# Bias table and first compress weights in 512 KB pieces, each behind a unit of the first sublayer

## The reference

```
for i in range(DEPTH):
    y = swiglu(rms_norm(h, g[0]), ffn_w_gate[i, 0], ffn_w_up[i, 0], ffn_w_down[i, 0])
    h = h + 0.5 * rms_norm(y, g[1])
    u = rms_norm(h, g[2])
    y = nsa_mixer(u, ..., rel_bias) if i % 2 == 0 else fox_mixer(u, ...)
    h = h + rms_norm(y, g[3])
    ... # second feed-forward sublayer, with g[4] and g[5]
```

## Time and profile before

| what | before |
|---|---|
| median of 3 runs | 1053.37 us (1052.19 to 1053.69) |
| the profiled execution | 1051.25 us |
| its span, first to last instruction | 1049.4 us |
| PE busy, share of the span | 98% |
| mean granted TensorE clock | 0.996 |
| HBM traffic over the span | 177 GB/s |

### The profile page before, as it was taken

One profiled execution on the slowest core, in us unless ns is written; L12 is line 12 of the kernel. 1 busy time (PEld: TensorE's weight loads), 2 busy tenths in 40 slices (PEclk: granted clock), 3 DMA queues, 4 the chain that ended last, 5 costly groups with the idle time before them and its releaser, 6 DMA issues.

```text
span 1049.4 us, 14401 instructions
## 1 busy us (share of the span) xinstructions
PE 1024.0 (98%) x5995; PEld 880.1 (84%) x5995; DVE 646.2 (62%) x777; ACT 517.7 (49%) x709; POOL 115.6 (11%) x219
## 2 busy tenths in 40 slices
PE   6989999999999999999999999999999999999997
PEld 6878888898866898888889888888988789888886
DVE  4646556656697665556575656556667775556554
ACT  4534444644465554444454444445554655444442
POOL 0100000222153200000020000001133420000000
PEclk9999999999999999999999999999999999999999
DMA  8694565568402365566556655655655145566552
GB/s 256 223 366 161 179 194 200 167 213 262 141 2 71 125 206 182 182 199 199 181 182 201 193 178 190 200 191 171 201 173 189 46 133 184 184 197 199 179 185 79
DMA packets 137830, 187.98 MB, mean 179 GB/s; under 512 B 7249, under 2 KB 120230, under 8 KB 137766
## 3 DMA queue, kind: packets, MB, share of 16 engines
q1 hardware_dynamic: 133702, 172.83, 50.9%
q0 software_dynamic: 3920, 14.18, 4.1%
q10 hardware_dynamic: 144, 0.07, 0.0%
HBM read 184.42 MB, written 1.07 MB: 177 GB/s over the span
## 4 chain that ended last, share of the span: by engine, by line
PE 88%; DVE 4%; DMA 2%; POOL 2%; ACT 2%; issue 2%; DVEq 0%; POOLq 0%; SPq 0%; ACTq 0%
PE ps L1117 85%; DMA raw<-in_ffn_w_gate 2%; PE ps L1456 1%; ACT work L527 1%; DVE normed L781 1%; POOL ms L402 1%; DVE wlo L746 1%; POOL rstd L404 1%; DVE res L770 1%; PE ps L1286 1%; DVE probT_buf L899 1%; POOL ms_half L398 0%; DVE normed L762 0%; DVE normed L877 0%; DVE wlo L738 0%
## 5 line engine op out<-in xcount | busy, mean ns | idle before, releaser
L738 DVE TENSOR_TENSOR wlo<-raw,whi 128x2048 fp32r<-128x2048 f32 x151 | 346.9, 2298 | 149.6 <-ACT whi L503 149.5
L1117 PE MATMUL ps<-xhl,whi 128*128 128x512 f32 (+1 forms) x1600 | 388.3, 385 | 3.4 <-DVE wlo L738 3.4
L1117 PEld LDWEIGHTS ps<-xhl,whi 128*128 128x128 f32 x1600 | 283.5, 189 | 54.7 <-issue 5.5
L503 ACT ACTIVATE whi<-raw 128x2048 fp32r<-128x2048 f32 x151 | 288.1, 1908 | 29.3 <-DMA raw<-in_ffn_w_gate 12.0
L1117 PEld LDWEIGHTS ps<-xhl,wlo 128*128 128x128 f32 x1600 | 216.5, 191 | 16.2 <-DVE wlo L746 1.7
L1117 PE MATMUL ps<-xhl,wlo 128*128 128x256 f32 (+1 forms) x1600 | 221.8, 282 | 0.9 <-DVE wlo L746 0.9
L1117 PE MATMUL ps<-whi,xhl 128*128 128x256 f32 (+1 forms) x640 | 136.1, 320 | 2.9 <-DVE xhl L789 2.9
L1117 PE MATMUL ps<-whi,hhi 128*128 128x512 f32 x320 | 124.9, 390 | 0.0
L1117 PE MATMUL ps<-wlo,hhi 128*128 128x512 f32 x320 | 124.9, 390 | 0.0
L1117 PE MATMUL ps<-whi,hlo 128*128 128x512 f32 x320 | 124.5, 389 | 0.0
L1117 PEld LDWEIGHTS ps<-whi,xhl 128*128 128x128 f32 x640 | 103.8, 193 | 12.3 <-DVE wlo L746 3.1
(11 more groups left out here) (169 smaller groups left out, 777.2 us busy)
## 6 DMA issues: line engine op xcount, KB each, us to landing
raw<-in_ffn_w_down SPq DMA_DIRECT2D x44, 1024.0 KB, 4.9
raw<-in_ffn_w_gate SPq DMA_DIRECT2D x41, 1024.0 KB, 5.3
raw<-in_ffn_w_up SPq DMA_DIRECT2D x41, 1024.0 KB, 5.4
raw<-in_fox_w_in SPq DMA_DIRECT2D x10, 1024.0 KB, 5.3
raw<-in_nsa_w_in SPq DMA_DIRECT2D x8, 1024.0 KB, 5.4
big<-in_nsa_cmp_w POOLq DMA_DIRECT2D x2, 2048.0 KB, 16.3
raw<-in_nsa_w_out SPq DMA_DIRECT2D x4, 1024.0 KB, 5.4
raw<-in_fox_w_out SPq DMA_DIRECT2D x4, 1024.0 KB, 4.7
```

The source lines that it names most:

```text
L503: nc.scalar.activation(whi[:, u % RING, :], raw_of(u), ACT.Copy).then_inc(w_hi, 1)
L738: nc.vector.tensor_tensor(wlo[:, u % RING, :], raw_of(u), whi[:, u % RING, :].bitcast(F32), ALU.subtract).then_inc(w_lo, 1)
L1117: return nc.tensor.matmul(out_, l, r, start=start, stop=stop)
```

## The change

POOL issues the two gain loads first, as soon as the scratch tensor has landed. The bias table is loaded in four pieces of four heads each (512 KB), piece b behind a wait for unit_done = 9, 11, 13, 15, and `w1` in four pieces of four row groups each (512 KB), behind unit_done = 17, 19, 21, 23. The two waits of the consumers count all four pieces.

```
             pool.wait_ge(vec_out, 16)
-            pool.dma_start(bias[:, :, :], bass.AP(scratch.tensor, 0, [[1, P], [SCORES, H], [1, S]])).then_inc(bias_in, 16)
             load_gain(0, 1)
             load_gain(1, 0)
-            pool.dma_start(w1, cmp_w1[0, 0].rearrange("(k p) n -> p k n", p=P)).then_inc(w1_in[0], 16)
+            for b in range(4):
+                pool.wait_ge(unit_done, 9 + 2 * b)
+                pool.dma_start(bias[:, 4 * b:4 * b + 4, :],
+                               bass.AP(scratch.tensor, 4 * b * SCORES, [[1, P], [SCORES, 4], [1, S]])).then_inc(bias_in, 16)
+            for b in range(4):
+                pool.wait_ge(unit_done, 17 + 2 * b)
+                pool.dma_start(w1[:, 4 * b:4 * b + 4, :],
+                               cmp_w1[0, 0][512 * b:512 * b + 512, :].rearrange("(k p) n -> p k n", p=P)).then_inc(w1_in[0], 16)
             between_sublayers(0)
...
                     def compressed_logits(r):
                         dve.wait_ge(sc_mm, r + 1)
-                        dve.wait_ge(bias_in, 16)
+                        dve.wait_ge(bias_in, 64)
...
             def compress_hidden(kv):
                 pe.wait_ge(flat_ready, kv + 1)
-                pe.wait_ge(w1_in[kv], 16)
+                pe.wait_ge(w1_in[kv], 16 if kv else 64)
```

## The result

The changed kernel takes 1046.09 us in the median of 6 runs (1046.0 to 1046.93), the kernel before 1052.95 in 6 runs (1050.06 to 1053.69); the ratio is 0.9941, 95% interval 0.9929 to 0.9952 (a ratio is formed over all the runs, so it is not the quotient of the two medians). The profiled execution went from 1051.25 to 1046.00 us, its span from 1049.4 to 1044.2.

What follows compares the result with a forecast made beforehand. PE sets the pace, busy in 98% of the span, but stalls for one late weight load. Idle time and slow clock, read together as 5.15 us, come off 1053.37, additions cost 0: 1048.2 us, range 1045.6 to 1050.8.

Steps and rivals of the forecast that it cites:

- The stall and its cause: First sublayer, before unit 10: POOL's 5 MB starve the ring, its load takes 15.56 us and PE idles 3.78 us.
- The yardstick of 11.8 us: Ring load of unit 10: harmless to PE if landed within 11.8 us of issue; a normal landing takes 5.3.
- The sum: Whole kernel: removing the stall saves 5.15 us, from 1051.25 to 1046.1 profiled and from 1053.37 to 1048.2 in the median.
- the clock, 1.51: First unit after the hole: PE at a mean granted clock of 0.84 takes 1.51 us more than the next unit.
- the lower bound of the range: Median: if its 2.12 us above the profiled execution were more of this stall, 7.3 us is gained, 1046.1.
- The gains on top of unit 8: Gain loads issued first, while unit 8's ring load is in flight: it lands at 8.1 us, inside 11.8, cost 0.
- The pieces beside the ring: Ring loads of units 12 to 26 issued with a piece: landing at 6.7 us, at worst 9.5, cost 0.
- The slower rival: Ring loads beside the eight pieces land after 11.8 us; at 13.0 the kernel takes 1057.8 us; chance 0.03.
- POOL's wait before the norm factors: POOL between sublayers: eighth piece issued about 146, norm factors wanted about 193, cover 47 us, cost 0.
- The price of small transfers: Eight pieces on POOL's queue: 25.6 us against 13.6 for two whole loads by the skill's estimate, where nobody waits, cost 0.

Runs made afterwards that it cites:

- e4: Kernel before with only w1, whole, moved behind unit_done 17; whole bias and gains at once as before; 1046.38 us, ratio 0.9946.
- e2: Kernel before with gains at once, the whole bias behind unit_done 9 and the whole w1 behind unit_done 17, no pieces; 1047.14 us, ratio 0.9955.
- e1: Kernel before with only the order changed: gains, then whole bias, then whole w1, no waits; 1052.13 us, ratio 1.0004.
- e3: Kernel before with bias and w1 each cut into four pieces, in the old order and without waits; 1052.72 us, ratio 1.0002.
- e8: Kernel before with only the two gains moved behind unit_done 9, leaving 4.2 MB queued at once; 1047.77 us, ratio 0.9955.
- e9: Kernel before plus one unread load of 0.79 MB behind w1 on POOL's queue, 6.0 MB in all; 1054.24 us, ratio 1.0022.
- e5_burst_at_unit_9: Kernel before with gains at once, then whole bias and whole w1 together behind unit_done 9, 4.2 MB; 1049.85 us, ratio 0.9979.
- the clock held: Kernel before with 15 small unread matmuls that PE runs in the hole before unit 10; 1050.07 us, ratio 0.998.
- e7: The changed kernel run again without edits, on a third chip; 1046.57 us, ratio 0.9944 against the kernel before.
- e6: Changed kernel with its eight pieces behind unit_done 9, 10 ... 16, one each unit; 1046.88 us, ratio 0.9945 against the kernel before.
- e11: Repeat of e2, whole bias and whole w1 behind unit_done 9 and 17, beside the changed kernel; 1046.42 us, ratio 0.9944.

## Why the prediction was right

The result lies in the stated range, and the mechanism held in all that has a price. The forecast of 1048.2 was 2.1 us above the result, though, and 1046.09 is at the very end of the forecast's own range (1046.1 to 1049.6): the size of the gain was put too low.

*The stall and its cause.* Right. It goes with the backlog (e4, e2) and stays with order and pieces changed (e1, e3). One reading was too general: that the ring gets a fifth of the bandwidth while POOL has work holds for gate and up units; the down unit 9 got half of it (the last section).

*The yardstick of 11.8 us.* Right. Landings of 9.7 (e4) did no harm; 13.14 (e8), 15.95 (e1) and 17.99 (e9) gave holes of 1.37, 4.17 and 6.20, each within 0.1 us of the landing less 11.8. In e5_burst_at_unit_9 it holds for unit 13 too: 14.57 and 2.79.

*The sum.* 5.15 us was right for the execution that it was read from: the profiled ones differ by 5.25. It was too small for the medians, 6.86 (6.6 in the repeat). The term that was too small for the medians is the clock, 1.51: with the clock held, 2.3 us came back. The prediction knew that the median of before was 2.12 over its profiled execution and carried the difference over to the changed kernel; that was the wrong choice, for it belonged to the stall, as the lower bound of the range had it. The changed kernel's median is 0.09 from its profiled run. Over the 59 runs of before beside the experiments the mean granted clock was 0.993 or less in 26, with a median of 1053.2, and 0.996 or more in 27, with a median of 1051.3. The changed kernel never showed less than 0.995 in its 11 runs. So the stall costs more or less clock from run to run; what decides it stays open. The hole itself differs less: 3.78, 4.17 and 4.01 us in the traces of before, e1 and e3.

*The gains on top of unit 8.* Right at no cost. Unit 8 landed after 5.4 us in the changed kernel and after 6.8 in its repeat; in two other kernels with the same order after 8.4 and 8.5 (I had 8.1), still without harm.

*The pieces beside the ring.* Right at no cost, wrong in the picture. I had the piece go first and the ring load land at 6.7; the ring loads landed after 4.9 to 5.6 and the pieces after 6.1 to 6.9. The queue tables of the changed kernel (packets, MB) show why, first from 70 to 72 us, then 72 to 73.5, for the piece issued at 69.00:

```profile
q1 hardware_dynamic: 137, 0.56, 72.2%
```

```profile
q1 hardware_dynamic: 121, 0.43, 70.2%
q0 software_dynamic: 50, 0.20, 33.1%
```

POOL's bytes begin to move only some 3 us after the issue, when SP's load of 68.73 is nearly through. A piece fits into the pause that a ring load leaves. The slower rival is ruled out by these landings and by the dense pieces.

*POOL's wait before the norm factors.* Right: 45.78 us of cover left, about 47 expected.

*The price of small transfers.* The 12 us more for eight pieces, estimated from the Trainium skill's DMA: Bandwidth & Descriptors, section Anatomy of one DMA, were never on the path: whole loads and pieces, both behind units, take 1046.42 and 1046.57. The traces here agree that pieces are dear for their size, and put more on a piece than the 3.2 us of that estimate: 6.1 to 6.9 us for 512 KB issued beside a ring load, against 11.1 for the 2 MB bias load of e2. The measurement decides.

## What to carry to other kernels

When one engine sets the pace and one load in its ring lands late, work out by when it must land (the pacing engine's start less the steps between) and then look at what else is queued on the DMA engines at its issue. Bytes that nobody needs for a long time should wait behind steps of the pacing engine, and not all behind the same one: here 2 MB behind a unit did no harm, 4.2 MB behind one made a hole of 2.79 us. Cutting the loads without the waits did not help. A hole of the matrix engine can cost more than its length, and here the surplus differed from run to run, so a single profiled execution can understate it.

## What was not expected of the hardware

POOL's loads move packets of 4 KB, and the ring's packets are of 1 KB for a gate or up unit: in the earlier trace rows 1.53 MB in 376 packets against 0.38 MB in 375. The packets of a down unit are of 4 KB. In the kernel before from 58 to 60 us, when the ring's bytes are those of the down unit 9, the counts are equal again, and now the bytes too:

```profile
q1 hardware_dynamic: 100, 0.41, 51.8%
q0 software_dynamic: 102, 0.40, 50.6%
```

Both tables fit queues that take turns by packets. A bulk load on POOL's queue takes four fifths of the bandwidth from a gate or up load that it meets and half from a down load, once both run. A ring load issued into the backlog also starts late: unit 13 of e5_burst_at_unit_9, issued at 73.92, moved no packet from 74 to 77.4, while POOL's moved 1.18 MB. And a POOL load behind a ring load starts late too (none of its bytes before 72, for an issue at 69.00). How much the ring load suffers hung on tenths of a us: with the two gain loads issued 0.11, 0.14, 0.27, 0.28, 0.38, 0.51 and 0.62 us behind the ring load of unit 8, it landed after 8.5, 8.4, 6.8, 6.1, 5.4, 5.4 and 5.4 us (e2, e5, e7, e6, the changed kernel, e1, e11). The mechanism behind this was not tested.

Over 70 to 90 us the clock had a mean of 0.91 with a hole of 3.78 us and of 0.83 with one of 6.20; after holes of 1.37 and 2.79 us it stayed at 1.00 in the profiled executions. In the trace with the hole of 6.20 it was 0.50 from 78 to 80, the 1.2 GHz level, when PE had stood still since 74.5. In the runs of e5_burst_at_unit_9 (hole 2.79 in its trace) the clock was 0.993 to 0.994 in 5 of 12, and these took 1050.9 to 1052.4 against 1048.4 to 1049.9 for the others.
